# Feed-forward up products with the weights stationary and both parts of x moving

## The reference

```python
h = h + jnp.square(jax.nn.relu(rms_norm(h, g) @ w_up)) @ w_down
```

## Time and profile before

| what | value |
|---|---|
| median of 3 runs | 2644.71 us (2642.17 to 2645.2) |
| profiled execution, its time | 2643.55 us |
| its span, first to last instruction | 2641.8 us |
| PE, DVE, ACT busy | 99%, 61%, 52% |
| weights read from HBM, mean rate | 460 MB, 177 GB/s |

### The profile page before, as it was taken

One profiled execution on the slowest core, in us unless ns is written; L12 is line 12 of the kernel. 1 busy time (PEld: TensorE's weight loads), 2 busy tenths in 40 slices (PEclk: granted clock), 3 DMA queues, 4 the chain that ended last, 5 costly groups with the idle time before them and its releaser, 6 DMA issues.

```text
span 2641.8 us, 31389 instructions
## 1 busy us (share of the span) xinstructions
PE 2602.6 (99%) x12510; PEld 2162.6 (82%) x12510; DVE 1612.8 (61%) x1938; ACT 1368.5 (52%) x1948; POOL 0.2 (0%) x4
## 2 busy tenths in 40 slices
PE   9999999999999999999899999999999999999998
PEld 7877888888888887887788888888888888888887
DVE  7685555555555556668788956544555555555555
ACT  6654544444444445668878754544544444444444
POOL 0000000000000000000000000000000000000000
PEclk9999999999999999999999999999999999999999
DMA  6543665566556654655444436543565665556554
GB/s 222 161 135 136 206 201 189 187 190 191 191 192 191 189 186 153 197 182 168 129 163 144 137 120 233 188 159 128 188 196 189 191 191 191 185 184 190 193 189 144
DMA packets 235529, 468.70 MB, mean 177 GB/s; under 512 B 8219, under 2 KB 17654, under 8 KB 234102
## 3 DMA queue, kind: packets, MB, share of 16 engines
q1 hardware_dynamic: 234246, 465.11, 54.0%
q10 hardware_dynamic: 1136, 1.58, 0.2%
HBM read 460.36 MB, written 6.29 MB: 177 GB/s over the span
## 4 chain that ended last, share of the span: by engine, by line
PE 49%; DVE 1%; ACT 1%; issue 0%; DVEq 0%; ACTq 0%
PE ps L168 47%; PE ps L172 2%; DVE XS L138 0%; ACT PRD L135 0%; DVE AC L138 0%; ACT WH L135 0%; DVE WL L138 0%; ACT QE L135 0%; DVE FO L145 0%; ACT SM L135 0%; ACT JK L135 0%; DVE H L138 0%; DVE QA L149 0%; DVE QE L149 0%; DVE QA L138 0%
## 5 line engine op out<-in xcount | busy, mean ns | idle before, releaser
L138 DVE TENSOR_TENSOR WL<-Wt,WH 128x1024 fp32r<-128x1024 f32 (+2 forms) x863 | 1042.6, 1210 | 796.3 <-ACT WH L135 761.6
L135 ACT ACTIVATE WH<-Wt 128x1024 fp32r<-128x1024 f32 (+2 forms) x863 | 900.0, 1045 | 787.6 <-PE ps L168 781.5
L168 PE MATMUL ps<-WH,XT 128*128 128x512 f32 (+1 forms) x3392 | 1085.2, 393 | 2.3 <-DVE XT L149 2.0
L168 PE MATMUL ps<-WH,HT 128*128 128x512 f32 (+2 forms) x3392 | 1059.9, 389 | 2.2 <-DVE WL L138 2.2
L168 PEld LDWEIGHTS ps<-WH,XT 128*128 128x128 f32 x3392 | 636.4, 188 | 132.5 <-DVE WL L138 2.2
L168 PEld LDWEIGHTS ps<-WH,HT 128*128 128x128 f32 x3392 | 635.3, 188 | 127.7 <-DVE WL L138 3.0
L168 PE MATMUL ps<-WL,XT 128*128 128x512 f32 (+1 forms) x1696 | 658.3, 388 | 0.0
L168 PE MATMUL ps<-WL,HT 128*128 128x512 f32 (+2 forms) x1696 | 654.3, 386 | 0.0
L168 PEld LDWEIGHTS ps<-WL,XT 128*128 128x128 f32 x1696 | 319.3, 188 | 62.1 <-issue 1.0
L168 PEld LDWEIGHTS ps<-WL,HT 128*128 128x128 f32 x1696 | 319.3, 188 | 61.5 <-issue 1.0
L138 DVE TENSOR_TENSOR H<-H,ps 128x512 f32<-128x512 f32 x144 | 92.8, 684 | 22.9 <-PE ps L168 22.9
(11 more groups left out here) (263 smaller groups left out, 1272.6 us busy)
## 6 DMA issues: line engine op xcount, KB each, us to landing
Wt<-in_mlp_w SPq DMA_DIRECT2D x128, 1024.0 KB, 5.3
Wt<-in_w_up SPq DMA_DIRECT2D x64, 1024.0 KB, 5.4
Wt<-in_w_down SPq DMA_DIRECT2D x64, 1024.0 KB, 5.0
Wt<-in_w_in SPq DMA_DIRECT2D x53, 1024.0 KB, 5.1
Wt<-in_w_out SPq DMA_DIRECT2D x32, 1024.0 KB, 5.1
Wt<-in_xa_wk SPq DMA_DIRECT2D x16, 1024.0 KB, 5.0
Wt<-in_xa_wv SPq DMA_DIRECT2D x16, 1024.0 KB, 5.0
Wt<-in_xa_wq SPq DMA_DIRECT2D x16, 1024.0 KB, 5.1
```

The lines of the kernel that those rows point to most:

```text
L135: return self.p.act.do(lambda e: e.activation(out, in_, func, **kw), w, self.name + "_a")
L138: return self.p.dve.do(lambda e: e.tensor_tensor(out, a, b, op), w, self.name + "_v")
L168: return self.p.pe.do(lambda e: e.matmul(out, l, r, start=start, stop=stop), w, self.name + "_t" if sig else None)
```

## The change

Up products get a function of their own, `gemm_t`. It keeps a block of 128x128 weights stationary and moves x. With the high weights it moves both parts of x at once: 512 columns, two runs of 256 from `XX[:, :, kt, :]`, which go to the two halves of one PSUM bank. With the low weights it moves the high part alone, 256 columns, into the bank's first half. Each of the four blocks of a chunk has a bank of its own, so a chunk holds four banks for its whole length: all of `G`, or all of the pool (u0: chunk 0 in `G`, chunk 1 in the pool; all others the other way round). Per half the order is block 0 with both rows of blocks, then block 1, and so on, with a signal after each.

The result has hidden rows on partitions and tokens along the free dimension, as the down product needs it. The transposes go. `ev_up` copies the bank's second half to `XL` (ACT, 256 columns) and adds the first half to it into `U` (DVE, 256 columns), four times; the bank is free after the addition. `turn` then squares with the ReLU from SBUF into `U2` (DVE, 2 of 512), copies the high part (ACT, 2 of 512) and takes the difference (DVE, 2 of 512).

The norm's factor belongs to a token and so can't be applied there any more; since relu(s a)^2 = s^2 relu(a)^2, its square is applied when the down result is added to `H`, by one DVE instruction that multiplies and adds.

```diff
+    def gemm_t(key, XX, xtok, evac):
+        k, chunks, segs = order[state["gemm"]]
...
+        for ci, ka, kb, _, _ in segs:
+            c0, w = chunks[ci]
+            if (ci == 0) == key.endswith("u0"):
+                sets = [(state["gset"], 0), (state["gset"], 1), (state["gset"] ^ 1, 0), (state["gset"] ^ 1, 1)]
+                own = [G[a][b][:, :] for a, b in sets]
+                own_free = [gfree[a][b] for a, b in sets]
...
+            else:
+                got = [banks.get() for _ in range(4)]
+                own, own_free = [g[1] for g in got], [g[2] for g in got]
...
+            for k2 in range(ka, kb, 2):
+                i = state["half"]
+                split_to(i + NR - 1)
+                state["half"] += 1
...
+                toks = []
+                for n in range(4):
+                    for kt in (k2, k2 + 1):
+                        o = (kt - k2) * w + n * P
+                        wh, wl = (t[:, i % NR, o:o + P] for t in (WH, WL))
+                        start, stop = kt == ka, kt == kb - 1
+                        both = (own[n].rearrange("p (a t) -> p a t", a=2), wh, XX[:, :, kt, :])
+                        one = (own[n][:, 0:256], wl, XX[:, 0, kt, :])
+                        ready = (split_tok[i], xtok[kt], own_free[n] if start else None)
+                        a, b = (both, one) if start else (one, both)
+                        st_g.mm(*a, ready, start=start, stop=False, sig=False)
+                        end = kt == k2 + 1
+                        tok = st_g.mm(*b, start=False, stop=stop, sig=end)
+                    toks.append(tok)
+                pe_free[i] = tok
+                running = list(bg)
+                if k2 == kb - 2:
+                    evac(ci, own, toks, give)
+                pump(running)
...
+                if factor is not None:
+                    res.append(st.stt(d, acc[tb], factor.r1[:, tb:tb + 1], d, MUL, ADD, tok, factor.ready()))
...
         def turn(u, e, ci, toks, free):
             b = e % 2
...
             for pr in range(2):
-                bi, bk, bf = banks.get()
-                for i in range(2):
-                    for tb in range(2):
-                        c = (2 * pr + i) * P
-                        t = st.tr(bk[:, i * 256 + tb * P:i * 256 + (tb + 1) * P], U2[:, u, tb, c:c + P], ident, toks,
-                                  bf, sig=(i == 1 and tb == 1))
+                x = fl(U[:, u, 2 * pr:2 * pr + 2, :])
+                v[pr] = st.stt(fl(U2[:, u, 2 * pr:2 * pr + 2, :]), x, 0.0, x, MAX, MUL, toks[2 * pr:2 * pr + 2], v_free[u])
+            u_free[u] = v
+            yield
+            for pr in range(2):
+                h[pr] = st.act(fl(hi[pr]), fl(U2[:, u, 2 * pr:2 * pr + 2, :]), ACT.Copy, v[pr], free)
+            yield
+            for pr in range(2):
+                h[pr] = st.tt(fl(lo[pr]), fl(U2[:, u, 2 * pr:2 * pr + 2, :]), fl(hi[pr]).bitcast(F32), SUB, h[pr], free)
...
-                for tb in range(2):
-                    r = st.act(U[:, u, tb, :], acc[tb], ACT.Relu, tok, u_free[u], norm.ready(),
-                               scale=norm.r1[:, tb:tb + 1])
-                    s = st.stt(U2[:, u, tb, :], acc[tb], 0.0, U[:, u, tb, :], MAX, MUL, r, u_free[u])
+                for i in range(4):
+                    a = st.act(XL[:, l, i, :], own[i][:, 256:512], ACT.Copy, toks[i], l_free[l])
+                    r = st.tt(U[:, u, i, :], own[i][:, 0:256], XL[:, l, i, :], ADD, a, toks[i], u_free[u])
+                    give(i, r)
+                    res.append(r)
...
-        gemm(f"{tag}u0", X, norm.done, ev_up(0))
-        ev_d = ev_h(f"evd{tag}")
+        gemm_t(f"{tag}u0", X, norm.done, ev_up(0))
+        ev_d = ev_h(f"evd{tag}", factor=norm)
...
-            r = st_l.tt(d, d, acc, ADD, tok)
+            r = st_l.stt(d, acc, n_m2.r1[:, tb:tb + 1], d, MUL, ADD, tok, n_m2.ready())
```

More of the change, by code:

```diff
@@ L389, in gemm, with give @@
                 return tok
+        return tok
+    def gemm_t(key, XX, xtok, evac):
+        k, chunks, segs = order[state["gemm"]]
+        assert k == key, (k, key)
+        state["gemm"] += 1
+        for ci, ka, kb, _, _ in segs:
[4 more added lines that the diff above has]
+                own_free = [gfree[a][b] for a, b in sets]
+                def give(n, tok, sets=sets):
+                    gfree[sets[n][0]][sets[n][1]] = tok
+            else:
+                got = [banks.get() for _ in range(4)]
+                own, own_free = [g[1] for g in got], [g[2] for g in got]
+                def give(n, tok, got=got):
+                    banks.free(got[n][0], tok)
+            for k2 in range(ka, kb, 2):
[3 more added lines that the diff above has]
+                for kt in (k2, k2 + 1):
+                    while xtok[kt] is None:
+                        assert bg
+                        pump()
+                toks = []
+                for n in range(4):
+                    for kt in (k2, k2 + 1):
+                        o = (kt - k2) * w + n * P
[14 more added lines that the diff above has]
+                pump(running)
         return tok
@@ L1083, in build, with ev_h @@
     t_hx = dma(p.sync, H[:, :, :], x_v, t_swa[0], sig="ld_x")
-    def ev_h(name, norm=None, scaled=None):
+    def ev_h(name, norm=None, scaled=None, factor=None):
         st = Stage(p, name)
@@ L1091, in evac @@
                 d = H[:, tb, c0:c0 + w]
-                if scaled is None:
+                if factor is not None:
+                    res.append(st.stt(d, acc[tb], factor.r1[:, tb:tb + 1], d, MUL, ADD, tok, factor.ready()))
+                elif scaled is None:
                     res.append(st.tt(d, d, acc[tb], ADD, tok, t_hx))
@@ L1108, in mlp @@
     def mlp(tag, norm, X, HB_, ev_last):
-        U = arena(f"U{tag}", [P, 3, 2, 512], 16384)
-        U2 = arena(f"V{tag}", [P, 3, 2, 512], 28672)
+        XL = arena(f"L{tag}", [P, 2, 4, 256], 8192)
+        U = arena(f"U{tag}", [P, 3, 4, 256], 16384)
+        U2 = arena(f"V{tag}", [P, 3, 4, 256], 28672)
         tok_hid = [[None] * 8, [None] * 8]
         hid_free = [None, None]
-        u_free = [None] * 3
+        u_free, v_free, l_free = [None] * 3, [None] * 3, [None] * 2
         st = Stage(p, f"hid{tag}")
@@ L1122, in turn @@
             b = e % 2
+            v, h = [None, None], [None, None]
+            fl = lambda t: t.rearrange("p a t -> p (a t)")
+            hi, lo = ([HB_[:, part, 8 * b + 4 * ci + 2 * pr:8 * b + 4 * ci + 2 * pr + 2, :] for pr in range(2)]
+                      for part in range(2))
             for pr in range(2):
-                bi, bk, bf = banks.get()
-                for i in range(2):
-                    for tb in range(2):
-                        c = (2 * pr + i) * P
-                        t = st.tr(bk[:, i * 256 + tb * P:i * 256 + (tb + 1) * P], U2[:, u, tb, c:c + P], ident, toks,
-                                  bf, sig=(i == 1 and tb == 1))
-                kt = 4 * ci + 2 * pr
[L1131 to L1136, removed]
+                x = fl(U[:, u, 2 * pr:2 * pr + 2, :])
[7 more added lines that the diff above has]
+                h[pr] = st.tt(fl(lo[pr]), fl(U2[:, u, 2 * pr:2 * pr + 2, :]), fl(hi[pr]).bitcast(F32), SUB, h[pr], free)
+                kt = 4 * ci + 2 * pr
+                tok_hid[b][kt] = tok_hid[b][kt + 1] = h[pr]
+            v_free[u] = h
+            yield
         def ev_up(e):
@@ L1140, in ev_up, with evac @@
             tok_hid[e % 2][:] = [None] * 8
-            def evac(ci, c0, w, acc, tok):
-                u = n[0] % 3
+            def evac(ci, own, toks, give):
+                u, l = n[0] % 3, n[0] % 2
                 n[0] += 1
-                toks, res = [], []
-                for tb in range(2):
-                    r = st.act(U[:, u, tb, :], acc[tb], ACT.Relu, tok, u_free[u], norm.ready(),
-                               scale=norm.r1[:, tb:tb + 1])
-                    s = st.stt(U2[:, u, tb, :], acc[tb], 0.0, U[:, u, tb, :], MAX, MUL, r, u_free[u])
[L1150 to L1153, removed]
-            return evac
-        gemm(f"{tag}u0", X, norm.done, ev_up(0))
-        ev_d = ev_h(f"evd{tag}")
+                res = []
+                for i in range(4):
[3 more added lines that the diff above has]
+                    res.append(r)
+                l_free[l] = res
+                bg.append(turn(u, e, ci, res, free))
+            return evac
+        gemm_t(f"{tag}u0", X, norm.done, ev_up(0))
+        ev_d = ev_h(f"evd{tag}", factor=norm)
         for e in range(8):
             if e < 7:
-                t_up = gemm(f"{tag}u{e + 1}", X, norm.done, ev_up(e + 1))
+                t_up = gemm_t(f"{tag}u{e + 1}", X, norm.done, ev_up(e + 1))
             hid_free[e % 2] = gemm(f"{tag}d{e}", lambda part, kt: hid(part, e % 2, kt), tok_hid[e % 2],
@@ L1172, in build @@
     n_mem = Norm("lnmem", lambda tb, c: MEM[:, tb, c * 512:(c + 1) * 512], KT, "norm_mem_g_2", xt, memx)
-    t_up, t_hid = mlp("m1", n_m1, ht, XT, ev_h("evlm1", n_mix))
```

(3 more changed lines are left out.)

## The result

The changed kernel takes 2634.14 us (median of 5 runs, 2633.68 to 2636.55) against 2643.64 us before (median of 5). The ratio is 0.9965, 95% interval 0.9952 to 0.9979: 9.5 us less, and the interval lies clear of no change. The forecast was 2630.5 us. The profiled execution took 2633.68 us with a span of 2631.7.

The account below looks back on a forecast made before the run. The prediction took PE's own sequence to bound the feed-forward layers: -30.9 (transposes) + 13.8 (added matmuls) + 4.0 (new wait) + 0.1 (last down sum) = -13.0 us, from 2643.55 to 2630.5 us, range 2619 to 2652.

Parts of the forecast that it names:

- The bound: In the feed-forward layers PE is never late for data, so the time is the sum of PE's own steps.
- What goes: 256 transposes on PE, in 64 groups at 0.48 us each, all of it path: -30.9 us.
- What PE gets: Up products: 8 matmuls and loads in place of 6 at 512 places, 13.5 ns per addition: +13.8 us; bounds -28 and +55.
- the last down sum: Down sums become product and sum on DVE; only the last lies behind the last matmul: +0.1 us.
- The new wait: PE waits 0.2 to 0.3 us for just-used PSUM banks at 16 hand-overs: +4 us; bounds 0 and +16.
- wrong if the hand-over is not near 0.25: Sign at the 16 hand-overs: the prediction is wrong if one does not cost PE near 0.25 us.
- Weight loads exposed: Rival in up products: a load needs more than the short step's 120 ns; 2657 us at 133, 2685 at 147; chance 0.13.
- the estimate of 2690 us: By the busy share of weight loads, 8 loads of 188 ns replace 1361 ns in 512 places: +73 us, sum +46.
- Second run costs an addition: Rival in the long step: the moving operand's second run costs 13.5 ns more, +28 us, 2658 us; chance 0.07.
- The wait takes the gain: Rival at the 16 hand-overs: 1.0 us each, sum -1, 2642.5 us, no change; chance 0.12.

Follow-up runs that it names:

- e4: The kernel before with its 64 groups of four transposes left out, so down products work on wrongly ordered values: 2611.54 us, ratio 0.988.
- e1: The changed kernel with all up products holding G in chunk 0 and the pool in chunk 1, so none starts in just-used banks: 2627.25 us, ratio 0.9938.
- e3: The changed kernel with the short step moving 192 columns in place of 256: 2629.51 us, ratio 0.9945.
- e0: The changed kernel as it is, run again on the chip of the second batch: 2634.44 us, ratio 0.9967 of the kernel before.
- e2: The changed kernel with the long step moving 512 columns in one run in place of two, with wrong operands: 2635.2 us, ratio 0.9967.
- e6: The changed kernel with the long step made as two of 256 columns, each with its own load, except in a chunk's first block: 2657.53 us, ratio 1.0055.
- e5: The changed kernel with the weight split in an up chunk's last half emitted behind the evacuation, no longer ahead of it: 2627.48 us, ratio 0.9938.

## Why the prediction was right, and where it was off

**The bound.** That PE's own sequence sets the time in the feed-forward layers was right. e4 took the transposes alone and got all of their time back. Nothing else took their place, with DVE and ACT doing as many pieces of the same size as before (their source is SBUF in place of a PSUM bank).

**What goes.** 30.9 us forecast, 30.9 measured by e4 in the feed-forward layers (31.7 as whole time, with the scatter of the rest). The price came from starts around a group and from a chunk, not from the busy rows (38.2 us for the 256 in the earlier trace rows).

**What PE gets.** +13.8 us forecast. An up product of e1 has 44.40 us where e4's has 43.52: 16 x 0.88 = 14.1 us. The feed-forward layers of e1 and e4 differ by 15.1 us. Of the last 1.0 us, 0.7 lie in u0 and u1 (90.12 against 88.01 us in each layer, where 0.88 each would give 1.8), and 0.3 behind the start of d6, where +0.1 was forecast for the last down sum. Their cause stays open; no run changes it. The law of columns plus a fixed addition held below the shortest step seen. The pair is 346.9 ns, forecast 347.0. The bounds in the forecast were far apart (-28 to +55 us), and the value was near neither. What made the choice was the pair of loads 0.11 us apart; e3 found the bound just below. One reading beside it was loose: the 126 ns of the float32 products are busy time alone (30.2 us for 240), and the 4.5 us idle before them in the earlier trace rows come on top.

**The new wait.** This is the term that was mis-sized: +4 us forecast, 6.8 measured (the feed-forward layers of the changed kernel less those of e1; 6.9 by their times). The place, the number and the cause (DVE in the split) were right, and the release came 0.19 us after PE could start, where 0.2 to 0.3 was forecast. Missing were the 0.11 us from the end of the sum to the first load, and that the load itself stands behind the wait and so is not hidden: the matmul starts 0.03 after it and its step takes 0.31 in place of 0.227. I had taken PE's start as the end of the sum. By its own sign ("wrong if the hand-over is not near 0.25") the prediction failed at this step, with 0.42.

**The sum again.** In the feed-forward layers, from before by way of e4 and e1 to the changed kernel: -30.9 + 15.1 + 6.8 = -9.0, rounded apart from the 8.9 measured (the three differences make up the whole by construction). The forecast was -13.0: 2.8 us of what is missing are in the hand-overs, 1.2 in what PE gets. The whole times give -9.5 and, in the later comparison (e0), -8.8.

**The rivals.** *Weight loads exposed*: did not happen, but by 3.4 ns a pair only; by e3 the loader is the likely bound just below. The Trainium skill (Perfetto Trace Analysis, Identifying the Most-Contended Engine) takes the busy share of the weight loads, beside the share of peak arithmetic, as the measure of headroom, and the estimate of 2690 us was made by it. Here it points at the right resource with the wrong size: in the up products 8 records of 188 ns make 1504 ns in 1390 ns of time, since they overlap. A record of 188 ns stands for 108 to 117 ns of the loader by the two readings of e3. *Second run costs an addition*: excluded by e2. The Trainium skill's rule that non-contiguous patterns slow matmuls (Advanced Engine Details and Errata, PSUM Cachelines) finds no support in e2 for two runs of 256 on the moving side; the output side was not tried. *The wait takes the gain*: it took 7 of 16 us (-30.9 + 15.1), less than the 16 that the rival put on the wait, and by DVE's late split, as that rival had it.

## What to carry to other kernels

Price a matmul by the distance of starts, as columns plus a fixed addition, and look for the shortest distance of two loads before making matmuls shorter; more, shorter matmuls were paid for here by the transposes that they made needless. When a change makes a stage hold all its banks to its end, let the next stage start in other banks, or emit the evacuation ahead of work that is not yet urgent on the same engine: either got back 7 us of the 16 here. Count for each such wait that comes late the signal and the first weight load behind it (0.23 us here), not only the release. Where the part of a program that no edit touches scatters by as much as the effect, compare the stage alone.

## What the runs showed of the hardware

- A float32r matmul with a load of its own takes N/2.4 ns + some 13 to 13.5 ns for N = 256, 320 and 512 columns (120.0 in e6, 146.8 in the earlier trace rows, 226.8 in the earlier trace rows); a pair of 256 and 512 in turn takes 346.9 ns, 13.5 on each (e1).
- Loads of 128x128 float32r weights are recorded with 188 ns but start as near as 108 ns to each other (e3). With 192 columns behind one with 512, the pair stops at 343 to 344 ns. The start of the matmul that waits for its weights is then recorded too early (0.09 us after the one before it), and the wait appears in its own step.
- A moving operand in two runs of 256 elements costs what one run costs (e2: 1432.5 us for the feed-forward layers either way).
- A matmul whose first load waits for a signal that comes late loses 0.23 us beyond the lateness: 0.11 to 0.12 to the load, 0.03 to the matmul, 0.08 in its step (four latenesses from 0.09 to 0.23 us in the changed kernel, e3 and e6). A signal that came 1.04 us early cost nothing (e5).
